# Sparse attention: one exponential for a pair's compressed scores, compressed keys in front of the selected keys, queries written straight into place

## The reference, cut to what matters

```python
q, kc, vc, ks, vs, kw, vw, gate, z = jnp.split(u @ w_in, points, axis=-1)
q = q.reshape(b, s, G, J, dh) * (dh ** -0.5)
...
k_cmp = compress(kc, pe_k, w1_k, w2_k)          # 31 compressed keys per group
v_cmp = compress(vc, pe_v, w1_v, w2_v)
...
s_c = einsum(q, k_cmp) + bias_c                 # compressed branch
p_c = softmax(where(m_c, s_c, NEG)) * any(m_c)
o_c = einsum(p_c, v_cmp)
s_s = einsum(q, k_g) + bias_s; o_s = einsum(softmax(s_s), v_g)   # selected keys
s_w = einsum(q, k_win) + bias_w; o_w = einsum(softmax(s_w), v_win) # window
o = gate[..., 0:1] * o_c + gate[..., 1:2] * o_s + gate[..., 2:3] * o_w
return (o * silu(z)) @ w_out
```

## Time and profile before

| | us |
|---|---|
| median of 3 runs (2043.79 to 2048.67) | 2044.93 |
| profiled execution | 2046.88 |
| its span | 2045.6 |
| PE, DVE, ACT, POOL busy | 2014.7, 1116.5, 818.5, 297.9 |
| PE on the chain that ended last | 91% |
| ACT, DVE on that chain | 5%, 3% |

### The profile page before, as it was taken

How to read it: one execution, slowest core, us unless ns; L and a number is a source line. 1 busy time by engine, 2 the same in 40 slices (tenths; PEclk the granted TensorE clock), 3 DMA queues, 4 the chain that set the end, 5 groups by cost and what they waited for, 6 DMA issues and landing times.

```text
span 2045.6 us, 26834 instructions
## 1 busy us (share of the span) xinstructions
PE 2014.7 (98%) x10045; PEld 1635.7 (80%) x10045; DVE 1116.5 (55%) x2227; ACT 818.5 (40%) x1610; POOL 297.9 (15%) x426
## 2 busy tenths in 40 slices
PE   8999999999999999999999999999998999999998
PEld 6887888888888886788888888888887888877776
DVE  5438435666684335435535666694436663635456
ACT  5226333333342222333323333343338884335453
POOL 1103100000001120000010000031004663212311
PEclk8999999999999999999999999999998999999999
DMA  5330142332334331132242332235321103423212
GB/s 172 105 102 12 62 132 88 104 103 78 98 113 135 94 102 42 52 97 99 62 137 90 108 106 77 91 114 161 124 96 39 33 22 104 122 77 104 73 42 83
DMA packets 96915, 186.82 MB, mean 91 GB/s; under 512 B 8424, under 2 KB 16656, under 8 KB 96658
## 3 DMA queue, kind: packets, MB, share of 16 engines
q1 hardware_dynamic: 90162, 163.31, 25.3%
q0 software_dynamic: 6352, 21.27, 3.3%
q10 hardware_dynamic: 272, 0.52, 0.1%
HBM read 180.81 MB, written 4.26 MB: 90 GB/s over the span
## 4 chain that ended last, share of the span: by engine, by line
PE 91%; ACT 5%; DVE 3%; issue 1%; DMA 0%; POOL 0%; SPq 0%; ACTq 0%; DVEq 0%; POOLq 0%
PE bank L819 54%; PE bank L875 9%; PE bank L912 8%; PE bank L1427 5%; PE bank L1188 2%; PE bank L1348 1%; PE bank L1325 1%; PE bank L1441 1%; PE bank L963 1%; ACT sc L2012 1%; PE bank L1173 1%; PE bank L993 1%; PE bank L1464 1%; ACT xn L2006 1%; PE bank L1082 1%
## 5 line engine op out<-in xcount | busy, mean ns | idle before, releaser
L2188 DVE TENSOR_TENSOR wl<-raw,wh 128x1024 fp32r<-128x1024 f32 x320 | 395.8, 1241 | 652.4 <-ACT wh L1548 651.5
L1548 ACT ACTIVATE wh<-raw 128x1024 fp32r<-128x1024 f32 x320 | 336.9, 1057 | 716.0 <-PE bank L819 593.4
L819 PE MATMUL bank<-hTh,wh 128*128 128x512 f32 x1184 | 461.1, 389 | 0.2 <-issue 0.2
L819 PE MATMUL bank<-hTl,wh 128*128 128x512 f32 x1184 | 460.8, 389 | 0.0
L819 PE MATMUL bank<-hTh,wl 128*128 128x512 f32 x1184 | 460.8, 389 | 0.0
L819 PEld LDWEIGHTS bank<-hTh,wh 128*128 128x128 f32 x1184 | 222.3, 188 | 46.6 <-issue 0.3
L819 PEld LDWEIGHTS bank<-hTh,wl 128*128 128x128 f32 x1184 | 222.3, 188 | 46.2
L819 PEld LDWEIGHTS bank<-hTl,wh 128*128 128x128 f32 x1184 | 222.3, 188 | 45.9
L819 PE MATMUL bank<-wh,hTh 128*128 128x512 f32 x400 | 156.6, 391 | 0.1
L819 PE MATMUL bank<-wh,hTl 128*128 128x512 f32 x400 | 155.7, 389 | 0.0
L819 PE MATMUL bank<-wl,hTh 128*128 128x512 f32 x400 | 155.7, 389 | 0.0
(11 more groups left out here) (427 smaller groups left out, 3462.6 us busy)
## 6 DMA issues: line engine op xcount, KB each, us to landing
raw<-in_ffn_w_in SPq DMA_DIRECT2D x88, 512.0 KB, 3.5
raw<-in_ret_w_in SPq DMA_DIRECT2D x48, 512.0 KB, 3.7
raw<-in_ffn_w_out SPq DMA_DIRECT2D x44, 512.0 KB, 3.7
raw<-in_diff_w_in SPq DMA_DIRECT2D x32, 512.0 KB, 3.6
raw<-in_fox_w_in SPq DMA_DIRECT2D x23, 512.0 KB, 3.6
raw<-in_nsa_w_in SPq DMA_DIRECT2D x20, 512.0 KB, 3.5
raw<-in_ret_w_out SPq DMA_DIRECT2D x16, 512.0 KB, 3.6
raw<-in_fox_w_out SPq DMA_DIRECT2D x8, 512.0 KB, 3.5
```

What stands on the lines that cost most here:

```text
L819: i = pe.do.matmul(dst, x, y, start=first and k == 0 and q == 0, stop=stop)
L1548: act.do.activation(M.hl[n % HL_SLOTS][0][:, 0:src.shape[1]], src, ACT.Copy).then_inc(*T.up("act_hi", n))
L2188: dve.do.tensor_tensor(wl[:, 0:m], src, wh[:, 0:m].bitcast(F32), ALU.subtract).then_inc(*T.up("dve_lo", n))
```

## The change

The compressed keys get 32 columns in front of the selected keys, in the same tile (`a.cs`, `a.csl`). For the query blocks i = 0, 1, 2 the compressed scores then come out of the matmuls of the selected branch, 32 columns longer (160, 288, 416), in the same bank; for i = 3, where the bank is full, `last_cmp_scores` makes them in bank 3, four matmuls of 32 columns per pair at step 2. DVE takes each tile's minimum right behind `largest`, subtracts the minima of both heads in one instruction at tile 7, ACT makes one exponential of 128 x 256 at tile 8, DVE sums and inverts at tile 10, POOL multiplies at tile 11 (two gate instructions and one product of 128 x 256), PE transposes both heads at step 12 (behind `turn` of tiles 6 and 7), ACT copies once. POOL fills the score buffer once with a large number, in place of DVE's two clearings.

`take_q` writes from PSUM to the queries' own partitions: two ACT and two DVE instructions per tile. The exponential's table is loaded by a small exponential ahead of the queries. The last split of the stage stands behind tile 16 of the attention loop.

The diff, cut to its core:

```diff
+            a.cs, a.csl = sb(stack, "kcs", [128, 4, 32 + S], F32R), sb(stack, "kcsl", [128, 4, 32 + S], F32R)
+            a.k = [a.cs[:, :, 32:32 + S], sb(stack, "kw", [128, 4, S], F32R)[:, :, :]]
+            a.kl = [a.csl[:, :, 32:32 + S], late_keys[:, :, :]]
...
-        if n % 8 == 4:
+        if n % 16 == 11:
             pool.wait_ge(*at("dve_gate", "any"))
-            pool.wait_ge(*at("dve_cmp", (h, "recip")))
-            pool.do.tensor_tensor(y[:, :, 2], y[:, :, 2], a.gate[:, :, 3 * h], ALU.mult).then_inc(*up("pool_cmp", (h, "gate")))
-            pool.wait_ge(*at("pool_cmp", (h, "gate")))
-            pool.do.tensor_tensor(x[:, :, 0:31], x[:, :, 0:31], y[:, :, 2:3].to_broadcast([128, 4, 31]), ALU.mult).then_inc(
-                *up("pool_cmp", (h, "weighed")))
+            pool.wait_ge(*at("dve_cmp", (t, "recip")))
+            for par in range(2):
+                y = a.scs[:, 4 * par:4 * par + 4, 2]
+                pool.do.tensor_tensor(y, y, a.gate[:, :, 3 * (2 * t + par)], ALU.mult).then_inc(*up("pool_cmp", (t, "gate")))
+            pool.wait_ge(*at("pool_cmp", (t, "gate")))
+            pool.do.tensor_tensor(a.cp[:, :, :], a.cp[:, :, :], a.scs[:, :, 2:3].to_broadcast([128, 8, 32]), ALU.mult).then_inc(
+                *up("pool_cmp", (t, "weighed")))
...
-    def cmp_scores(h):
+    def last_cmp_scores(t):
...
+        qs = slice(3 * 128, 4 * 128)
+        for par in range(2):
+            h, out = 2 * t + par, M.bank[3][:, par * 32:par * 32 + 32]
+            pe.do.matmul(out, query(M, h)[:, qs], a.cs[:, h // 4, 0:32], start=True, stop=False)
+            pe.do.matmul(out, query(M, h)[:, qs], a.csl[:, h // 4, 0:32], start=False, stop=True).then_inc(*up("pe_cmp", ("scores", h)))
+        pe.free[3] = [("dve_cmp", (2 * t + par, 3, "max")) for par in range(2)]
...
-        pe.free[b] = [("dve_max", ("nsa", n))]
+        pe.wait_ge(*at("act_kcmp", "hi"))
+        pe.wait_ge(*at("dve_kcmp", "lo"))
+        qs, pe.free[b] = slice(i * 128, i * 128 + 128), [("dve_max", ("nsa", n))]
+        if beside(n):
+            x, y = a.cs[:, g, 0:32 + L], a.csl[:, g, 0:32 + L]
+            pe.free[b].append(("dve_cmp", (h, i, "max")))
+        else:
+            x, y = a.k[br][:, g, 0:L], a.kl[br][:, g, 0:L]
+        dst = M.bank[b][:, 0:x.shape[1]]
...
+        if n % 16 == 7:
             pe_bank(pe, T, 3)
-            pe.wait_ge(*at("pool_cmp", (h, "weighed")))
-            pe.do.transpose(M.bank[3][:, 0:128], a.sc[h % 2][:, :, :].rearrange("p i c -> p (i c)"), M.ident[:, :]).then_inc(
-                *up("pe_cmp", ("turned", h)))
-            pe.free[3] = [("act_pc", h)]
+            pe.wait_ge(*at("pool_cmp", (n // 16, "weighed")))
+            for par in range(2):
+                t = pe.do.transpose(M.bank[3][:, par * 128:par * 128 + 128], a.cp[:, 4 * par:4 * par + 4, :].rearrange("p i c -> p (i c)"), M.ident[:, :])
+            t.then_inc(*up("pe_cmp", ("turned", n // 16)))
+            pe.free[3] = [("act_pc", n // 16)]
...
-        if p % 8 == 0 and p < 128:
-            cmp_scores(p // 8)
+        if p % 16 == 2 and p < 128:
+            last_cmp_scores(p // 16)
...
         def take(o):
-            t, b = base + o, o % 2
-            r = 64 * (t // 2 % 2)
-            hi = M.xn[0][:, b * S:b * S + S]
+            t = base + o
             act.wait_ge(*at("pe_product", (f"nsa q{base}", o)))
-            act.wait_ge(*at("pe_cmp", ("hidden", 1)))
-            if t >= 2:
-                act.wait_ge(*at("act_q", t - 2))
-                act.wait_ge(*at("dve_q", t - 2))
-                act.wait_ge(*at("dve_qlo", t - 2))
-            act.do.activation(hi.bitcast(F32R), M.bank[bank[f"nsa q{base}"][o]][:, :], ACT.Copy, scale=0.125).then_inc(*up("act_qhi", t))
-            act.wait_ge(*at("act_qhi", t))
             for par in range(2):
-                act.do.activation(query(M, 2 * t + par)[r:r + 64, :], hi[64 * par:64 * par + 64, :], ACT.Copy).then_inc(*up("act_q", t))
+                own = slice(64 * par, 64 * par + 64)
+                act.do.activation(query(M, 2 * t + par)[own, :], M.bank[bank[f"nsa q{base}"][o]][own, :], ACT.Copy, scale=0.125).then_inc(
+                    *up("act_q", (t, par), t))
...
+    act.wait_ge(*at("pool_cell", "power"))
+    act.do.activation(M.smalls[:, 1, 3:4], M.smalls[:, 0, 3:4], ACT.Exp).then_inc(*up("act_ahead", "table"))
     act_product(act, T, M, 4, 4, take_q(0))
-    act_product(act, T, M, 4, 4, take_q(4))
+    act_product(act, T, M, 3)
+    for o in range(4):
+        take_q(4)(o)
...
-        if n % 8 == 2:
-            h = n // 8
-            act.wait_ge(*at("dve_cmp", (h, "max")))
-            for i in range(4):
-                x, y = a.sc[h % 2][:, i, 0:cmp_blocks(i)], a.scs[h % 2][:, i, :]
-                act.do.activation(x, x, ACT.Exp, bias=y[:, 0:1], scale=-1.0, accum_out=y[:, 1:2]).then_inc(*up("act_cmp", h))
+        if n % 16 == 8:
+            act.wait_ge(*at("dve_cmp", (n // 16, "below")))
+            act.do.activation(a.cp[:, :, :], a.cp[:, :, :], ACT.Exp, scale=-1.0).then_inc(*up("act_cmp", n // 16))
...
+        if n == 16:
+            act_split(act, T, M)
...
+            t = base + o
             for par in range(2):
-                dve.do.tensor_copy(query(M, 2 * t + par)[64 - r:128 - r, :], lo[64 * par:64 * par + 64, :]).then_inc(*up("dve_q", t))
+                own, other = slice(64 * par, 64 * par + 64), slice(64 - 64 * par, 128 - 64 * par)
+                q = query(M, 2 * t + par)
+                dve.wait_ge(*at("act_q", (t, par)))
+                dve.do.scalar_tensor_tensor(out=q[other, :], in0=M.bank[bank[f"nsa q{base}"][o]][own, :], scalar=0.125,
+                                            in1=q[own, :].bitcast(F32), op0=ALU.mult, op1=ALU.subtract).then_inc(*up("dve_q", t))
...
+        if br == 0:
+            dve.wait_ge(*at("pool_blank", "scores"))
+            if i == 3:
+                dve.wait_ge(*at("pe_cmp", ("scores", h)))
+            k, src = cmp_blocks(i), M.bank[n % 3] if beside(n) else M.bank[3]
+            c = 0 if beside(n) else h % 2 * 32
+            bias = bass.AP(tensor=a.BT[h % 4][:, :].tensor, offset=96 + 128 * i, ap=[[512, 128], [-16, k]])
+            m = 4 * (h % 2) + i
+            dve.do.tensor_tensor_reduce(a.sc[:, m, 0:k], src[:, c:c + k], bias, -1.0, BIG, ALU.add, ALU.min,
+                                        a.scs[:, m, 0:1]).then_inc(*up("dve_cmp", (h, i, "max")))
+        if n % 16 == 7:
+            t = n // 16
+            for par in range(2):
+                dve.wait_ge(*at("dve_cmp", (2 * t + par, 3, "max")))
+            if t:
+                dve.wait_ge(*at("pe_cmp", ("turned", t - 1)))
+            dve.do.tensor_tensor(a.cp[:, :, :], a.sc[:, :, :], a.scs[:, :, 0:1].to_broadcast([128, 8, 32]), ALU.subtract).then_inc(
+                *up("dve_cmp", (t, "below")))
+        if n % 16 == 10:
+            t = n // 16
+            dve.wait_ge(*at("act_cmp", t))
+            dve.do.reduce_sum(a.scs[:, :, 1], a.cp[:, :, :], AX.X).then_inc(*up("dve_cmp", (t, "sum")))
+            dve.wait_ge(*at("dve_cmp", (t, "sum")))
+            dve.do.reciprocal(a.scs[:, :, 2], a.scs[:, :, 1]).then_inc(*up("dve_cmp", (t, "recip")))
...
+        if n == 16:
+            dve_split(dve, T, M)
```

More of the change, by code:

```diff
@@ L432, in nsa_tile, with beside @@
     return n // 16 * 2 + n % 2, n % 16 // 8, n % 8 // 2
+def beside(n):
+    return n % 16 < 6
 def nsa_dve(n):
@@ L684, in pool_nsa @@
         load_bt(h)
+    pool.wait_ge(*at("pe_cmp", "values"))
+    for w in range(2):
+        pool.wait_ge(*at("act_hid", w))
+    pool.do.memset(a.sc[:, :, :], BIG).then_inc(*up("pool_blank", "scores"))
     def weigh(n):
@@ L694, in scores @@
     def scores(n):
-        h = n // 8
-        x, y = a.sc[h % 2], a.scs[h % 2]
+        t, h = n // 16, n // 8
         if n % 16 == 3 and 2 <= h < 14:
@@ L1290, in pe_nsa @@
         pe_product(pe, T, M, f"nsa q{base}", "F", 8, h_, ready, 512,
-                   lambda o: [("act_qhi", base + o), ("dve_qlo", base + o)])
+                   lambda o: [("act_q", base + o), ("dve_q", base + o)])
     T.note("pe", "nsa heads")
-    def cmp_scores(h):
+    def last_cmp_scores(t):
         pe_bank(pe, T, 3)
-        pe.wait_ge(*at("act_kcmp", "hi"))
-        pe.wait_ge(*at("dve_kcmp", "lo"))
-        for i in range(4):
[L1299 to L1303, removed]
+        qs = slice(3 * 128, 4 * 128)
[4 more added lines that the diff above has]
+        pe.free[3] = [("dve_cmp", (2 * t + par, 3, "max")) for par in range(2)]
     def scores(n):
@@ L1312, in scores @@
         pe.wait_ge(*at("dve_k", 2 * br + g // 2))
[L1313 to L1316, removed]
-        pe.free[b] = [("dve_max", ("nsa", n))]
+        pe.wait_ge(*at("act_kcmp", "hi"))
[7 more added lines that the diff above has]
+        dst = M.bank[b][:, 0:x.shape[1]]
+        pe.do.matmul(dst, query(M, h)[:, qs], x, start=True, stop=False)
+        pe.do.matmul(dst, query(M, h)[:, qs], y, start=False, stop=True).then_inc(*up("pe_score", ("nsa", n)))
```

(32 more changed lines are left out.)

40 lines of the change are left out of this document (8 added, 32 removed).

## The result

The changed kernel takes 2048.69 us (median of 20 runs, 2045.56 to 2049.29), the kernel before 2044.16 (20 runs). The ratio is 1.0013 with a 95% interval of 1.0007 to 1.0019: about 2.7 us slower, by less than the 0.3% that was called no change, but on the other side of it than forecast (4 us faster). The medians lie 4.5 us apart and the means 2.8, because the executions of each kernel fall into groups some us apart, and the median sits in the largest one. The profiled execution of the changed kernel took 2046.77 us.

A forecast was written before the change was run, and what follows sets the result against it. PE was taken to hold 91% of the chain, with ACT's work keeping it from using the removed matmuls' time. Terms -8.8 + 2.6 + 1.8 = -4.4 us gave 2041 us, range 2031 to 2049.

The forecast's parts named there:

- Term 2: Second pair of the attention loop: the split moved behind tile 16 delays PE's turn, +2.6 us once, bounds 0 to 2.7.
- Term 1: Boundary from queries to attention loop, and first pair: first minimum 3.9 us earlier, second pair 9.3 earlier; -8.8 us with clock charge.
- Its other bound, -4: Boundary and first pair: gain of only 4 us if the clock stays low as long as before.
- The bound of -9.4: Boundary and first pair: gain of 9.4 us if the clock does not fall.
- Term 3: Seven steady pairs: 19.0 instead of 18.74 us each, as PE waits for ACT's copies and POOL's product; +1.8 us.
- the third: Attention loop: POOL is late, product 1.27 us, pairs 19.6, clock low as long as before; +4.6 us, 2050; chance 0.12.

The follow-up runs named there:

- the one with the later turn: The changed kernel with the turn of the compressed weights, and ACT's copy of it, two tiles later: 2043.99 us, ratio 0.9998 to the kernel before.
- filled wait: The changed kernel with eleven matmuls of 512 columns into an unread bank on PE, ahead of the turn that waits in the second pair: 2043.65 us.
- second trace of before: The kernel before the change, unchanged, traced once more: 2043.43 us.
- the three together: The changed kernel with copies ahead of exponentials, large exponential one tile later, compressed turn two later, and the split where its engines idle: 2034.72 us, ratio 0.9949.
- second trace of the changed kernel: The changed kernel, unchanged, traced once more: 2048.43 us.

## Why the prediction was wrong

**Term 2 failed: "+2.6 us, once", with bounds from 0 to 2.7.** The place, the chain and the wait were right (2.67 us on PE, turn at 4.95 into the pair, 5.0 forecast). The price was not: the second pair is 5.6 us longer than a steady one. The step left out is that this idle stretch takes TensorE's clock down (in all three traces that have the wait: two of the changed kernel, and the one with the later turn), and that PE, with DVE and ACT idle from 1565 to 1567, then works at 1.2 GHz for 6.8 us. The filled wait shows it: 3.0 of the 5.6 are the clock. The prediction had the row for it, as it weighed such a fall at the boundary and not here.

**Term 1 was too large: -8.8 forecast.** It is even the larger miss in us, where like executions are compared: -4.7 instead of -8.8, and +5.6 instead of +2.6. The first minimum came 3.03 us after the loop's start, 2.3 forecast: DVE's eight rests take 0.71 each, without the overlap that was subtracted from them. Against the trace shown, the first pair gained 7.33; against the second trace of before, 22.79 - 18.06 = 4.73. The prediction took the 14 us at 1.2 GHz of one profiled execution for the kernel's habit, though it saw that this execution lay 2 us above the median and took 1.5 us off for that. Its other bound, -4, is nearer to what was measured, but by luck: it stands for a clock that stays low as long as in the trace shown, and in the two traces of the changed kernel it was low for 3.4 and 6.8 us. (The bound of -9.4 is 9.3 by its own figures, 1566.07 less 1556.8.) The 1.28 of the table load, counted as gone, was worth 0.4 at most: the first eight tiles are paced by DVE and ACT together, and such a delay is caught up within them.

**Term 3 was right in its sum, in part by luck, and mostly in its parts.** Pairs of 18.98 us, 19.0 forecast, but 9.79 and 9.19 by half, where 9.6 and 9.4 were forecast: two errors of 0.2 that cancel. In the selected half the 0.2 for the compressed turn were not saved: from the turn at 1644.48 to the half's end it is 4.81, 4.64 forecast. The waits came, those for the copies with 0.25 and 0.39 (0.27 and 0.29 forecast), in the window half 0.49 and 0.39 (0.6 and 0.3), last compressed scores 1643.64 - 1643.18 = 0.46 (0.5). Too long was the wait for POOL, 0.33 instead of 0.65: the product took 0.63 us (0.7), and the rounding rest started 3.13 after the half's start, as ACT's rounding came 0.26 later, not 0.35. PE itself came to that turn 5.7 us into the half, 5.5 forecast:

```profile
1652.42 1.28 POOL L723 TENSOR_TENSOR qn<-prodn,qn 128x512 fp32r<-128x512 f32 x1 [0.98 <-ACT qn L2040]
...
1654.54 0.63 POOL L715 TENSOR_TENSOR cp<-cp,scs 128x256 f32<-128x256 f32 x1
```

The large exponential lasts 0.40 us in this pair, and ACT's next instruction starts 0.31 us after its start (1650.50 and 1650.81); 0.36 was taken for that step. The estimate of 0.31 from the Trainium skill (ScalarE: Activation LUTs, What ACT_TABLE_LOAD costs), 186 ns and 0.833 ns per column less an overlap of 93 ns, agrees with it. That PE could not use the 0.93 per half holds: with one reordering a pair falls from 18.98 to 18.64 or 18.77, and only with the three together to 18.01.

**The sum again, from like executions:** -4.7 for the first pair (second trace of before), +5.6 in the second, and (18.99 - 18.77) x 7 = +1.5 for the others, where both figures are means over the full pairs behind them: +2.4 us. These two executions, however, differ by 2046.77 - 2043.43 = 3.3 us. The other 0.9 lie behind the last matmul and are in no term: SP waits 2.6 us for the last transfer of the output to land, 1.7 before. All eleven traces of the changed kernel and its variants show 2.5 or 2.6, both traces of before 1.7; why is not shown. The ratio over all executions says 2.7 (1.4 to 3.9).

**Of the rivals,** the third had the sign, but neither its place nor its mechanism: POOL's product was short (0.63 us), and the low clock of the first pair was not its price. None put the clock's fall behind the moved split.

## What to carry to other kernels

Work that is moved off a boundary into a loop bound by TensorE should stand where its engine idles in that loop: behind tile 16 the same two instructions cost 5.6 us, behind tiles 11 and 15 nothing that can be seen. Price an idle stretch of TensorE with the slow stretch that may follow, and check on a second trace whether a slow stretch belongs to the kernel or to one execution. Removing matmuls between two waits shows up as longer waits, until the engine that they hid is reordered too.

## What the runs showed of the hardware

The clock does not fall in every execution behind the same idle stretch: 1.45 us of waiting at 1916 to 1918 were followed by 1.2 GHz in one execution of the changed kernel and not in another. So it was with PE's wait at the start of the loop, about 2.7 us in both: from 1543 to 1549 the granted clock was 1.00 in the first trace and 0.50 in the second. And what a fall costs depends on who paces: in the first pair 6.8 us at 1.2 GHz from 1543 left the pair at 18.0 us (second trace of the changed kernel), as long as 3.4 us from 1549 (its first), and 3.4 us from 1545 at 17.1 (the filled wait): DVE and ACT pace the first eight tiles, and there a slow PE is partly hidden: they took 8.41 us in the second trace, with 1.2 GHz from 1543 on, and 6.71 in the first, all of it at 2.4 GHz. In the second pair, 6.8 us at 1.2 GHz cost 3.0.
